# Where the rwkv operands are made beside gated linear attention: key norms, sigmoids, decays and the output gate moved

## The chip, the cores and the metric

The kernel runs on one core of a Trainium2 chip. The metric is the device time of one execution in microseconds (us). TensorE does the matrix products, VectorE (DVE) and ScalarE (ACT) the elementwise work, GpSimd (POOL) a few elementwise products, SyncE the loads of weights.

## The reference, cut to what matters

Two layers of attention and retention, a feed-forward block, a token mixer of four parts (pool, hgrn, rwkv, gla), and a second feed-forward block, over 512 tokens of 1024 features, all in float32. The change touches the token mixer, in the parts rwkv and gla:

```python
rr, rk, rv, xw, xa, xg = split(p_rw + (prev - p_rw) * rwkv_mu)
w_log = -softplus(-(rwkv_w0 + tanh(xw) @ rwkv_w2)) - 0.5
decay = exp(-exp(w_log))
a = sigmoid(rwkv_a0 + xa @ rwkv_a2)
g_r = sigmoid(xg) @ rwkv_g2
kk = split_heads(rk * rwkv_k_k)
kk = kk / maximum(sqrt(sum(kk * kk, -1)), 1e-12)
rk = rk * (1.0 + (a - 1.0) * rwkv_k_a)
# rwkv: S = S diag(decay) - (S kk)(kk * a)^T + v k^T, o = S r, token by token
# gla: o = chunked_gated_linear_attention(gq * scale, gk, gv, log_a), normed per head
y_gla = o_g * gla_norm * silu(gg)
```

The kernel computes the rwkv recurrence in chunks of 64 tokens, with the inverse of a triangular matrix per chunk and head. For it every key is scaled with the decays from the start of its chunk, which are exponentials of a running sum of `sigma`, the sigmoid of the low-rank product.

## The kernel before

Each engine has its own program; semaphores with names tie them. The order of the work is written out by hand. A weight arrives as a unit (512 or 384 KB) in one of 4 raw slots; ScalarE writes its high part (`w_high`, "weights high") and VectorE the rest (`w_low`, "weights split"), 3 slots each; `use()` keeps these splits 3 units ahead of the products. TensorE does three passes per product (L497 to L499).

The mixers' stage runs pool, hgrn and gla first. `linear_attention` (L840 on TensorE, L1591 on VectorE, L2267 on ScalarE) builds the scores of a chunked attention level by level, in `ORDER` = 32, 16, 8, 4, 2, 1, 64, 128, 256. For each level VectorE writes the logs of a factor (`logs`), ScalarE takes their exponential (`factor`), VectorE multiplies (`factors`), TensorE makes the scores (`scores`), and VectorE copies them with a mask (up to 64) or ScalarE copies them (`far`, levels 128 and 256). Between levels `fill(n)` does other work. Behind the last level come the mixed products, scores by values, whose results ScalarE lands in `y_gla`; then it presets X and XT, and the inverse begins.

In gla, `fill_gla` makes the eight rwkv projections between the first levels (0 to 5). VectorE lands each (`rwkv landed`) and mixes it with the token before (`rwkv mixed`), ScalarE keeps the own part (`rwkv own`). From the seventh fill on, `operand_steps` (L945, L1764, L2397) makes the rwkv operands: tanh, low-rank products, key squares and key norms; the four sigmoids; GpSimd's power -0.5 of the norms (L2657); the norms spread and turned; the scans of sigma (`cum`), the exclusive sum `cum - sigma`, three exponentials, and then `kkE`, `bI`, `kI` and `rE`. `bend_gate("gla")` (L2319) takes the silu of gla's output gate, between two exponentials.

`keep_busy(n)` makes n products that nobody reads. A PSUM bank is taken in turn out of 8; `take` waits until its user before is done.

Of the kernel before, what the change touches and what calls it, by code (L numbers as in the profile page):

```python
# [76 lines left out]
for _sem, _names in (  # L77
        ("rwkv operands by T", "sigma in,a gate in,gate out,key norm,key turned,bonus in,tokA turned,tokB turned"),
        ("rwkv operands by S", "rwkv tanh,rwkv sigmoid,sigma,a gate,g tok,key squares,key spread,rwkv exps,rwkv fades,bonus,tokA,tokB,"
                               "rwkv own,X preset,XT preset"),  # L80
        ("rwkv operands by V", "key floored,key scaled,sigma summed,sigma before,rE,rwkv landed,rwkv mixed"),
        ("inverse by T", "AT product,X product,A_ak product,Gv product,M_rk product,M_rb product,W1 product,"
                         "W2T product,X step,XT step,Pm product"),
        ("inverse by V", "X made,AT,X,XT made,A_ak,M_rk,M_rb,W2T"),
        ("inverse by S", "Pm,Gv,W1")):
    SHARED_BY.update((_name, _sem) for _name in _names.split(","))
# [103 lines left out]
class Memory:  # L190
# [80 lines left out]
    def mixers(self, region, rotary_at, xg_at, phase_at, end):  # L271
# [9 lines left out]
        m.y_tok = {name: r.room(f"y_{name}", TT, G) for name in ("hgrn", "rwkv", "gla")}  # L281
        first_at = r.at
# [167 lines left out]
def tensor_engine(e, s, mem, units):  # L450
# [371 lines left out]
    def mixers():  # L822
# [17 lines left out]
        def linear_attention(name, fill):  # L840
# [41 lines left out]
            for n in range(len(ORDER)):  # L882
                if n + 1 < len(ORDER):
                    fill(n + 1)
                if name == "gla" and n == len(ORDER) - 1:
                    keep_busy(3)
                scores(n)
# [57 lines left out]
        def operand_steps():  # L945
            yield
            for f in range(2):
                for what, r in (("sigma", slice(0, 64)), ("a gate", slice(64, 128))):
                    i = take((what, f), (what, f))
                    p.wait_ge(*of("rwkv tanh"))  # L950
                    group(banks[i][:, :], [(m.lora[r, 0, blk(f)], m.mixed[r, 6, :])], what + " in", f)
# [6 lines left out]
            yield  # L958
# [6 lines left out]
            for f in range(2):  # L965
                i = take(("key turned", f), ("key scaled", f))
                p.wait_ge(*of("key spread"))
                transposes(i, [flat(m.kI)[:, blk(2 * t + f)] for t in range(TT)], "key turned", f)
            yield
            yield  # L970
            yield

        projections, operand_prep = rwkv_steps(), operand_steps()

        def fill_gla(n):
            if n < 2:
                next(values_g)
                next(projections)
            elif n < 6:
                next(projections)  # L980
                if n in (2, 4):
                    next(projections)
                if n == 5:
                    p.mark("xg read", MIX_NORM)
            else:
                next(operand_prep)

        linear_attention("gla", fill_gla)
        for _ in operand_prep:
            pass  # L990
# [228 lines left out]
def vector_engine(e, s, mem, units):  # L1219
# [359 lines left out]
    def mixers():  # L1579
# [11 lines left out]
        def linear_attention(name, fill, mix):  # L1591
# [69 lines left out]
            def finish():  # L1661
                squares = groups_of(flat(k2 if name == "hgrn" else mem.square), G)
                v.wait_ge(*of("mixed landed", name, 1))
# [9 lines left out]
                v.wait_ge(*of("gate bent", name))  # L1673
                tt(y, y, v2[:, :, G:], ALU.mult, "y made", name)
# [68 lines left out]
        finish_hgrn = linear_attention("hgrn", fill_hgrn, lambda n: None)  # L1743
# [19 lines left out]

        def operand_steps():  # L1764
            yield
            norms = small[:, 176:192]
            v.wait_ge(*of("key norm"))
            ts(norms, bank("key norm")[:, 0:16], 1e-24, None, ALU.max, ALU.bypass, "key floored")
            yield
            v.wait_ge(*of("sigma", 1))  # L1770
            for f in range(2):
                scan(m.cum[:, f, :], m.sigma[:, f, :], "sigma summed", f)
            tt(m.tmp, m.cum, m.sigma, ALU.subtract, "sigma before")
# [4 lines left out]
            yield  # L1778
# [6 lines left out]
            yield  # L1785
# [6 lines left out]
            yield  # L1792
            tt(m.kI, rk, eI, ALU.mult, *STEP)
            v.wait_ge(*of("rwkv fades"))
            tt(m.rE, rr, m.eB, ALU.mult, "rE")
            yield

        projections, operand_prep = rwkv_steps(), operand_steps()

        def fill_gla(n):  # L1800
            if n < 6:
# [5 lines left out]
                if n in (2, 4):  # L1807
                    next(projections)
                    next(projections)
            else:  # L1810
                next(operand_prep)
# [5 lines left out]
        finish_gla = linear_attention("gla", fill_gla, mix_gla)  # L1817
        for _ in operand_prep:
            pass
# [3 lines left out]
    def inverse(m, finish_gla):  # L1823
# [37 lines left out]
        for size in (2, 4, 8, 16, 32):  # L1861
# [7 lines left out]
            for h in HEADS:  # L1869
# [4 lines left out]
                update("XT", m.XT[:, h, :], True, h)  # L1874
            next(side, None)
# [111 lines left out]
def scalar_engine(e, s, mem, units, t):  # L1987
# [273 lines left out]
    def mixers():  # L2261
# [5 lines left out]
        def linear_attention(name, fill):  # L2267
# [29 lines left out]
            for n in range(len(ORDER)):  # L2297
# [3 lines left out]
                elif name == "gla":  # L2301
                    fill(n + 1)
                scores(n)
            if name == "hgrn":
                fill(len(ORDER))
# [83 lines left out]
        def rwkv_steps():  # L2389
            for f in range(8):  # L2390
                use()
# [5 lines left out]
        def operand_steps():  # L2397
            a.wait_ge(*of("rwkv mixed", 7))
            act(m.mixed[0:64, 6, :], m.mixed[0:64, 6, :], "rwkv tanh", func=ACT.Tanh)
            a.wait_ge(*of("xg read", MIX_NORM))  # L2400
            for f in range(2):
                act(m.kI[:, f, :], m.mixed[:, 2 + f, :], "key squares", func=ACT.Square, scale=mem.col("rwkv_k_k", f))
            yield
            for f in range(2):
                for what, out, bias in (("sigma", m.sigma, "rwkv_w0"), ("a gate", m.a_gate, "rwkv_a0")):
# [3 lines left out]
            a.wait_ge(*of("key norm"))  # L2409
            a.wait_ge(*of("key inverse"))  # L2410
            act(heads(flat(m.kI)), small[:, 176:192].unsqueeze(2).to_broadcast([P, 16, 64]), "key spread")
            yield
# [4 lines left out]
            yield  # L2417
            a.wait_ge(*of("sigma before"))
            act(m.tmp, m.tmp, *STEP, func=ACT.Exp, scale=-HALF_E)
            act(m.rE, m.cum, "rwkv exps", func=ACT.Exp, scale=HALF_E)  # L2420
            act(m.eB, m.cum, "rwkv fades", func=ACT.Exp, scale=-HALF_E)
            yield
            yield

        projections, operand_prep = rwkv_steps(), operand_steps()

        def fill_gla(n):
# [5 lines left out]
            elif n < 6:  # L2433
                next(projections)
                if n in (2, 4):
                    next(projections)
            else:
                next(operand_prep)
            if n == 4:
                bend_gate("gla")  # L2440
# [8 lines left out]
        for _ in operand_prep:  # L2449
            pass  # L2450
# [5 lines left out]
    def inverse(m, finish_gla):  # L2456
# [21 lines left out]
        for size in (2, 4, 8, 16, 32):  # L2478
# [7 lines left out]
            for h in HEADS:  # L2486
                if h + 2 < 4:
                    product(h + 2)
                else:
                    next(side, None)  # L2490
            next(side, None)
# [85 lines left out]
def gpsimd_engine(e, s, mem, t):  # L2577
# [56 lines left out]
    def mixers():  # L2634
# [22 lines left out]
        tt(norms, norms, root, ALU.pow, "key inverse")  # L2657
        inverse(m)
# [208 lines left out]
```

## Time and profile before

| | us |
|---|---|
| median of 3 runs | 1688.22 |
| lowest and highest run | 1681.46, 1688.24 |
| profiled execution, its own time | 1687.16 |
| its span in the profile | 1685.2 |
| TensorE busy in the span | 1650.3 |
| VectorE busy | 861.3 |
| ScalarE busy | 669.0 |
| GpSimd busy | 124.7 |

The span runs from the first to the last instruction recorded; the time holds 1.96 us more. An engine is busy while it computes; what stands in square brackets at the end of a row is the time it stood idle just before, and who released it. Times within the trace count from the span's start. The stage of the change lies between 1090 and 1240 us.

### The profile page before, as it was taken

Reading aid. Unit: us, or ns where it says so; the run is one execution under the profiler, and the core shown is the slowest. Engines: PE = TensorE matmul, PEld = TensorE weight load, DVE = VectorE, ACT = ScalarE, POOL = GpSimd, SP = SyncE. Lnnn points to the kernel's source line nnn. Section 1 sums busy time; section 2 is a strip of 40 time slices with the busy share of each in tenths; the row PEclk is TensorE's granted clock in tenths of the full one; section 3 lists DMA queues with packets and bytes.
Section 4 is the critical chain, followed back from the end, with each engine's and each line's share of the span. In section 5 each row is a group of like instructions: output and inputs, shape, how many; then the busy total and the mean of one; then the engine's idle time right before and its main releaser. Section 6 shows DMA issues by size and latency. Waiting matters only on the chain.

```text
span 1685.2 us, 23809 instructions
## 1 busy us (share of the span) xinstructions
PE 1650.3 (98%) x9540; PEld 1338.2 (79%) x9540; DVE 861.3 (51%) x1170; ACT 669.0 (40%) x1017; POOL 124.7 (7%) x126
## 2 busy tenths in 40 slices
PE   9999999999999999999999999998999999999997
PEld 6877778877777888888888878887877888888886
DVE  6733445542444565444433478577556554444333
ACT  6145565314656433233222355346333433333221
POOL 0001001000100110000000310000410200000000
PEclk9999999999999999999999999997899999999999
DMA  5412212331221223332233422220002232232331
GB/s 180 154 63 76 88 51 88 113 125 63 75 77 53 98 85 103 100 101 90 88 103 94 141 76 63 63 66 18 3 23 86 88 101 92 96 97 85 103 98 56
DMA packets 40750, 144.14 MB, mean 86 GB/s; under 512 B 4816, under 2 KB 4832, under 8 KB 40256
## 3 DMA queue, kind: packets, MB, share of 16 engines
q1 hardware_dynamic: 37296, 131.61, 24.7%
q0 software_dynamic: 2192, 8.87, 1.6%
q10 hardware_dynamic: 1152, 2.14, 0.4%
q8 instruction: 76, 1.25, 0.3%
q14 instruction: 34, 0.28, 0.1%
HBM read 140.50 MB, written 2.10 MB: 85 GB/s over the span
## 4 chain that ended last, share of the span: by engine, by line
PE 85%; DVE 8%; ACT 5%; issue 1%; POOL 0%; DMA 0%; DVEq 0%; ACTq 0%; SPq 0%; POOLq 0%
PE bank L497 25%; PE bank L499 24%; PE bank L498 24%; PE bank L479 3%; PE bank L1017 2%; PE bank L485 1%; DVE sb_w_low L1230 1%; PE bank L664 1%; PE bank L728 1%; PE bank L707 1%; ACT sb_w_high L1999 1%; DVE sb_E L1230 1%; PE bank L862 1%; DVE sb_near L1644 1%; DMA sb_x<-xT 0%
## 5 line engine op out<-in xcount | busy, mean ns | idle before, releaser
L1230 DVE TENSOR_TENSOR sb_w_low<-sb_raw,sb_w_high 128x1024 fp32r<-128x1024 f32 (+1 forms) x253 | 310.9, 1229 | 368.0 <-ACT sb_w_high L1999 361.5
L497 PE MATMUL bank<-sb_xg_high,sb_w_high 128*128 128x512 f32 x1176 | 465.6, 396 | 2.0 <-DVE sb_w_low L1230 1.4
L499 PE MATMUL bank<-sb_xg_high,sb_w_low 128*128 128x512 f32 x1176 | 459.0, 390 | 0.0
L498 PE MATMUL bank<-sb_xg_low,sb_w_high 128*128 128x512 f32 x1176 | 458.5, 390 | 0.0
L1999 ACT ACTIVATE sb_w_high<-sb_raw 128x1024 fp32r<-128x1024 f32 (+1 forms) x253 | 263.3, 1041 | 349.1 <-PE bank L499 325.1
L497 PEld LDWEIGHTS bank<-sb_xg_high,sb_w_high 128*128 128x128 f32 x1176 | 221.1, 188 | 65.3 <-issue 15.8
L499 PEld LDWEIGHTS bank<-sb_xg_high,sb_w_low 128*128 128x128 f32 x1176 | 221.0, 188 | 47.1
L498 PEld LDWEIGHTS bank<-sb_xg_low,sb_w_high 128*128 128x128 f32 x1176 | 221.3, 188 | 44.3 <-issue 0.2
L499 PE MATMUL bank<-sb_h_high,sb_w_low 128*128 128x512 f32 x352 | 136.9, 389 | 0.0
L497 PE MATMUL bank<-sb_h_high,sb_w_high 128*128 128x512 f32 x352 | 136.9, 389 | 0.0
L498 PE MATMUL bank<-sb_h_low,sb_w_high 128*128 128x512 f32 x352 | 136.9, 389 | 0.0
L497 PE MATMUL bank<-sb_w_high,sb_xg_high 128*128 128x512 f32 x256 | 103.2, 403 | 0.0
L498 PE MATMUL bank<-sb_w_low,sb_xg_high 128*128 128x512 f32 x256 | 100.3, 392 | 0.0
L499 PE MATMUL bank<-sb_w_high,sb_xg_low 128*128 128x512 f32 x256 | 100.0, 391 | 0.0
L2586 POOL TENSOR_TENSOR sb_square_sum<-sb_square_sum,sb_square 128x512 f32<-128x512 f32 x20 | 26.1, 1307 | 748.4 <-ACT sb_square L1999 748.4
L499 PEld LDWEIGHTS bank<-sb_h_high,sb_w_low 128*128 128x128 f32 x352 | 66.1, 188 | 13.8
L498 PEld LDWEIGHTS bank<-sb_h_low,sb_w_high 128*128 128x128 f32 x352 | 66.1, 188 | 13.8
L497 PEld LDWEIGHTS bank<-sb_h_high,sb_w_high 128*128 128x128 f32 x352 | 66.1, 188 | 13.5
L1999 ACT ACTIVATE sb_h_high<-sb_up 128x512 fp32r<-128x512 f32 x44 | 27.8, 632 | 115.8 <-DVE sb_up L1230 115.8
L1230 DVE TENSOR_TENSOR sb_up<-bank,sb_inv_rms 128x512 f32<-128x512 f32 x44 | 30.4, 691 | 78.2 <-PE bank L499 77.4
L1999 ACT ACTIVATE sb_gate<-sb_gate 128x512 f32<-128x512 f32 x44 | 27.8, 632 | 92.3 <-DVE sb_gate L1230 92.3
L497 PEld LDWEIGHTS bank<-sb_w_high,sb_xg_high 128*128 128x128 f32 x256 | 48.3, 189 | 17.1 <-issue 7.1
(343 smaller groups left out, 1995.4 us busy)
## 6 DMA issues: line engine op xcount, KB each, us to landing
sb_raw<-w_ffn_in SPq DMA_DIRECT2D x88, 512.0 KB, 3.5
sb_raw<-w_ffn_out SPq DMA_DIRECT2D x32, 512.0 KB, 3.5
sb_raw<-w_tok SPq DMA_DIRECT2D x24, 512.0 KB, 3.5
sb_raw<-w_mix_f SPq DMA_DIRECT2D x18, 512.0 KB, 3.5
sb_raw<-w_rot SPq DMA_DIRECT2D x16, 512.0 KB, 3.6
sb_raw<-w_qk SPq DMA_DIRECT2D x16, 512.0 KB, 3.4
sb_raw<-w_out SPq DMA_DIRECT2D x16, 512.0 KB, 3.5
sb_raw<-w_ffn_out SPq DMA_DIRECT2D x16, 384.0 KB, 3.1
```

Of the source, the lines that this page charges most:

```text
L479: made = e.matmul(out, lhsT, rhs, start=n == 0, stop=n == len(pairs) - 1)
L485: made = e.transpose(banks[i][:, blk(n)], in_, mem.ident)
L497: e.matmul(out, w[0], v[0], start=first, stop=False)
L498: e.matmul(out, w[0], v[1], start=False, stop=False)
L499: return e.matmul(out, w[1], v[0], start=False, stop=last)
L664: made = e.matmul(out[k], m.feat["rk"][r, f, blk(j)], m.feat["rq"][r, f, j * P:], start=part == 0, stop=part == 1)
L707: e.matmul(out[k], m.qT[r, j, blk(q)], m.kT[r, j, 0:keys], start=True, stop=True).then_inc(*p.up("scores", n, 2 * j + k, q))
L728: made = e.matmul(out[64 * k:64 * k + 64, blk(q)], m.tok["av"][:, key, h * ATT_DIM:(h + 1) * ATT_DIM], m.probT[:, 2 * (q % 2) + k, blk(key ...
L1017: made = e.matmul(out(banks[i], t, c), left(t, c), right(t, c), start=True, stop=True)
L1230: e.tensor_tensor(out, a, b, op).then_inc(*v.up(*signal))
L1999: e.activation(out, in_, func, bias=bias, scale=scale, accum_out=accum).then_inc(*a.up(*signal))
L2586: e.tensor_tensor(out, a, b, op).then_inc(*g.up(*signal))
```

## The change

The operands are made at other places. Key squares, key norms and GpSimd's power move from the fills of levels 64 and 1 into the projections (fill 4), the spread to fill 5. They use the memory of `y_rwkv`. TensorE turns the keys just ahead of the scores of level 256, with two keep-busy products in place of three. All sigmoids, gla's output gate among them, stand in fill 6; its silu becomes a sigmoid on ScalarE and a product on GpSimd. The scans of sigma stand between the logs and the factors of level 128; the exclusive decay is the inclusive one of the token before, so that one subtraction and one exponential go and a small copy for the first token of each chunk comes. VectorE makes all the operands in fill 8. The products of rwkv's output gate go behind the scores of level 256. Two splits of weights move from projections 6 and 7 into the inverse, behind sizes 4 and 8 on VectorE, 2 and 4 on ScalarE.

```diff
@@ TensorE
-                if name == "gla" and n == len(ORDER) - 1:
-                    keep_busy(3)
+                if before_last and n == len(ORDER) - 1:
+                    before_last()
+                    keep_busy(2)
...
+        def key_norms():
             i = take(("key norm",), ("key floored",))
             p.wait_ge(*of("key squares"))
             for t in range(TT):
                 for f in range(2):
                     at = 4 * t + 2 * f
-                    group(banks[i][:, at:at + 2], [(m.kI[:, f, blk(t)], mem.table("same_head")[:, 0:P:64])], "key norm")
+                    group(banks[i][:, at:at + 2], [(m.key_sq[:, f, blk(t)], mem.table("same_head")[:, 0:P:64])], "key norm")
+
+        def turn_keys():
+            for f in range(2):
+                i = take(("key turned", f), ("key scaled", f))
+                p.wait_ge(*of("key spread"))
+                transposes(i, [flat(m.key_sq)[:, blk(2 * t + f)] for t in range(TT)], "key turned", f)
...
             elif n < 6:
                 next(projections)
+                if n == 4:
+                    key_norms()
                 if n in (2, 4):
                     next(projections)
...
+            elif n == 6:
+                low_rank_gates()
+            elif n == 9:
+                output_gate()
+
+        linear_attention("gla", fill_gla, turn_keys)
@@ VectorE
+                between(n)
                 if n + 1 < len(ORDER):
                     factors(n + 1)
                     fill(n + 1)
...
-                use()
+                if f < 6:
+                    use()
                 v.wait_ge(*of("rwkv", f))
...
+        def sum_sigmas(n):
+            if n == 6:
+                for f in range(2):
+                    v.wait_ge(*of("sigma", f))
+                    scan(m.cum[:, f, :], m.sigma[:, f, :], "sigma summed", f)
...
-            tt(m.tmp, m.cum, m.sigma, ALU.subtract, "sigma before")
...
+            v.wait_ge(*of("rwkv fades"))
+            tt(out[:, :, 1:], keys[:, :, 1:], fades[:, :, 0:CHUNK - 1], ALU.mult, *STEP)
+            ts(out[:, :, 0:1], keys[:, :, 0:1], 1.0, None, ALU.mult, ALU.bypass, *STEP)
             v.wait_ge(*of("a gate", 1))
             v.wait_ge(*of("rwkv exps"))
-            tt(m.kkE, kk, m.tmp, ALU.mult, *STEP)
...
+            elif n == 8:
+                operand_steps()
...
+            if size in (4, 8):
+                use()
@@ ScalarE
-            act(gate, gate, "gate bent", name, func=ACT.Sigmoid if name == "hgrn" else ACT.Silu)
+            if name == "hgrn":
+                act(gate, gate, "gate bent", name, func=ACT.Sigmoid)
+            else:
+                act(m.gate_sigmoid, gate, "gate sigmoid", func=ACT.Sigmoid)
...
+                if n == 5:
+                    low_rank_tanh()
+                    spread_norms()
                 next(projections)
+                if n == 3:
+                    square_keys()
...
+            elif n == 6:
+                sigmoids()
+            elif n == 7:
+                raise_decays()
+            elif n == 9:
+                land_gate()
...
+            if size in (2, 4):
+                use()
@@ GpSimd
         tt(norms, norms, root, ALU.pow, "key inverse")
+        gate = m.operands["gla"][3][:, :, G:]
+        g.wait_ge(*of("gate sigmoid"))
+        tt(gate, gate, m.gate_sigmoid, ALU.mult, "gate bent", "gla")
```

## Rows read from the trace of the kernel before

**Rows 1.** Span and busy totals of the page.

```profile
span 1685.2 us, 23809 instructions
...
PE 1650.3 (98%) x9540; PEld 1338.2 (79%) x9540; DVE 861.3 (51%) x1170; ACT 669.0 (40%) x1017; POOL 124.7 (7%) x126
```

**Rows 2.** Busy time per stretch: five engines, TensorE clock as share of 2.4 GHz, DMA.

```profile
1147.00:1149.00 2.00, 0.18 (x4) 0.04 (x2) 1.86 (x3) 0.92 (x2) 0.00 (x0) 0.86 0.08 29
...
1157.00:1165.00 8.00, 8.00 (x45) 7.04 (x45) 3.54 (x6) 6.17 (x8) 3.44 (x1) 0.50 0.01 2
...
1166.00:1171.00 5.00, 3.95 (x23) 2.03 (x22) 4.72 (x5) 2.78 (x6) 0.00 (x0) 1.00 0.01 2
...
1186.00:1189.00 3.00, 3.00 (x16) 3.00 (x16) 1.37 (x4) 2.43 (x6) 0.73 (x1) 0.50 0.00 0
...
1197.00:1203.00 6.00, 6.00 (x130) 6.00 (x132) 3.35 (x6) 1.14 (x3) 1.30 (x2) 0.50 0.01 3
```

**Rows 3.** TensorE in order of time, 1143 to 1175: start, duration, line, operation.

```profile
1143.39 3.79 PE L862 MATMUL bank<-sb_E 64*128 64x64 f32 x64
1150.21 3.78 PE L479 MATMUL bank<-sb_mixed,sb_lora 64*128 64x512 f32 x8 [3.03 <-ACT sb_mixed L1999]
1153.92 3.57 PE L479 MATMUL bank<-sb_mixer,sb_kI 128*128 128x2 f32 x16
...
1161.04 3.78 PE L479 MATMUL bank<-sb_lora,sb_mixed 128*128 128x256 f32 x8
...
1166.02 1.16 PE L873 MATMUL bank<-sb_E 64*128 64x128 f32 x16
1167.11 2.84 PE L813 MATMUL bank<-sb_inv_rms,sb_ones 128*128 128x512 f32 x6
1171.22 2.00 PE L876 MATMUL bank<-sb_E 64*128 64x256 f32 x16 [1.26 <-DVE sb_bI L1238]
```

**Rows 4.** Chain of work that ended last, 1157 to 1184: start, duration, what.

```profile
1157.88 3.45 POOL sb_small L2586
...
1174.27 8.89 PE bank L479 x80
```

**Rows 5.** TensorE in order of time, behind the mixed products.

```profile
1185.31 1.28 PE L479 MATMUL bank<-sb_mixer,sb_sigma 128*128 128x2 f32 x8
...
1192.01 0.38 PE L485 MATMUL bank<-sb_shared,sb_kkE 128*128 128x128 f32 x2
```

**Rows 6.** VectorE in order of time, 1134 to 1182.

```profile
1134.95 0.96 DVE L1230 TENSOR_TENSOR sb_w_low<-sb_raw,sb_w_high 128x768 fp32r<-128x768 f32 x1 [0.21 <-ACT sb_w_high L1999]
...
1142.29 1.53 DVE L1230 TENSOR_TENSOR sb_E<-sb_E,sb_kq_gla 128x1024 f32<-128x1024 f32 x1 [1.05 <-ACT sb_E L1999]
...
1144.99 0.69 DVE L1230 TENSOR_TENSOR sb_shifted<-bank,sb_inv_rms 128x512 f32<-128x512 f32 x1
...
1153.56 2.63 DVE L1644 COPY_PREDICATED sb_near<-sb_mixer,bank 128x512 f32<-128x512 int32 x2
...
1166.48 2.48 DVE L1250 TENSOR_TENSOR_SCAN sb_cum<-sb_mixer,sb_sigma 128x512 f32<-128x512 f32 x2
...
1170.32 1.60 DVE L1238 SCALAR_TENSOR_TENSOR sb_bI<-sb_mixed,sb_cols,bank 128x512 f32<-128x512 f32 x2
...
1181.66 1.23 DVE L1230 TENSOR_TENSOR sb_rE<-sb_mixed,sb_eB 128x1024 f32<-128x1024 f32 x1
```

**Rows 7.** ScalarE in order of time, around the output gate's silu.

```profile
1137.47 1.28 ACT L1999 ACT_TABLE_LOAD   x1
```

**Rows 8.** GpSimd in order of time, the inverse stage.

```profile
1225.85 2.35 POOL L2586 TENSOR_TENSOR sb_g_tok<-sb_g_tok,sb_rows 128x1024 f32<-128x1024 f32 x1
```

**Rows 9.** VectorE in order of time, while GpSimd builds pooling sums.

```profile
962.80 2.08 DVE L1230 TENSOR_TENSOR sb_w_low<-sb_raw,sb_w_high 128x1024 fp32r<-128x1024 f32 x1
...
967.55 1.23 DVE L1230 TENSOR_TENSOR sb_w_low<-sb_raw,sb_w_high 128x1024 fp32r<-128x1024 f32 x1 [1.87 <-ACT sb_w_high L1999]
```

**Rows 10.** GpSimd in order of time, the same stretch.

```profile
960.73 5.30 POOL L2586 TENSOR_TENSOR sb_s<-sb_s 128x1050 f32<-128x1050 f32 x3
```

More of the change, by code:

```diff
@@ L80 @@
                                "rwkv own,X preset,XT preset"),
-        ("rwkv operands by V", "key floored,key scaled,sigma summed,sigma before,rE,rwkv landed,rwkv mixed"),
+        ("rwkv operands by V", "key floored,key scaled,sigma summed,rE,rwkv landed,rwkv mixed"),
         ("inverse by T", "AT product,X product,A_ak product,Gv product,M_rk product,M_rb product,W1 product,"
@@ L281, in mixers @@
         m.y_tok = {name: r.room(f"y_{name}", TT, G) for name in ("hgrn", "rwkv", "gla")}
+        m.key_sq = flat(m.y_tok["rwkv"]).rearrange("p (f n) -> p f n", f=2)
+        m.gate_sigmoid = self.square.rearrange("p f (a b) -> p (f a) b", b=G)
         first_at = r.at
@@ L943, in rwkv_steps @@
                 yield
[L945 to L951, printed above, removed]
+        def key_norms():
             i = take(("key norm",), ("key floored",))
@@ L956, in operand_steps, with low_rank_gates, output_gate @@
                     at = 4 * t + 2 * f
-                    group(banks[i][:, at:at + 2], [(m.kI[:, f, blk(t)], mem.table("same_head")[:, 0:P:64])], "key norm")
-            yield
+                    group(banks[i][:, at:at + 2], [(m.key_sq[:, f, blk(t)], mem.table("same_head")[:, 0:P:64])], "key norm")
[4 more added lines that the diff above has]
+                transposes(i, [flat(m.key_sq)[:, blk(2 * t + f)] for t in range(TT)], "key turned", f)
+        def low_rank_gates():
+            for what, r in (("sigma", slice(0, 64)), ("a gate", slice(64, 128))):
+                for f in range(2):
+                    i = take((what, f), (what, f))
+                    p.wait_ge(*of("rwkv tanh"))
+                    group(banks[i][:, :], [(m.lora[r, 0, blk(f)], m.mixed[r, 6, :])], what + " in", f)
+        def output_gate():
             for half in range(2):
@@ L964, in operand_steps @@
                           "gate out", half)
[L965 to L973, printed above, removed]
+        projections = rwkv_steps()
         def fill_gla(n):
@@ L984, in fill_gla @@
                     p.mark("xg read", MIX_NORM)
[L985 to L990, printed above, removed]
+            elif n == 6:
[3 more added lines that the diff above has]
+        linear_attention("gla", fill_gla, turn_keys)
         p.mark("TensorE at", "inverse")
@@ L1589, in mixers, with linear_attention @@
             tt(m.p_in[:, f, m.pad:], bank("pool in", f)[:, :], mem.inv_rms, ALU.mult, "pool in landed", f)
-        def linear_attention(name, fill, mix):
+        def linear_attention(name, fill, mix, between):
             q2, k2, c2, v2 = m.operands[name]
@@ L1662, in finish @@
                 squares = groups_of(flat(k2 if name == "hgrn" else mem.square), G)
+                v.wait_ge(*of("gate bent", name))
                 v.wait_ge(*of("mixed landed", name, 1))
@@ L1672, in finish @@
                 tt(split(y), split(y), ms.unsqueeze(2).to_broadcast([P, n_norms, width]), ALU.mult, *STEP)
-                v.wait_ge(*of("gate bent", name))
                 tt(y, y, v2[:, :, G:], ALU.mult, "y made", name)
@@ L1762, in mixers, with floor_norms @@
         rr, rk, kk, eI = m.mixed[:, 0:2, :], m.mixed[:, 2:4, :], m.bI, m.rE
-        def operand_steps():
[L1765 to L1772, printed above, removed]
-            tt(m.tmp, m.cum, m.sigma, ALU.subtract, "sigma before")
+        def floor_norms():
+            v.wait_ge(*of("key norm"))
+            ts(small[:, 176:192], bank("key norm")[:, 0:16], 1e-24, None, ALU.max, ALU.bypass, "key floored")
+        def sum_sigmas(n):
+            if n == 6:
+                for f in range(2):
+                    v.wait_ge(*of("sigma", f))
+                    scan(m.cum[:, f, :], m.sigma[:, f, :], "sigma summed", f)
+        def operand_steps():
             for f in range(2):
@@ L1791, in operand_steps @@
                 stt(m.sigma[:, f, :], rr[:, f, :], mem.col("rwkv_r_k", f), rk[:, f, :], ALU.mult, ALU.mult, *STEP)
-            yield
             tt(m.kI, rk, eI, ALU.mult, *STEP)
-            v.wait_ge(*of("rwkv fades"))
             tt(m.rE, rr, m.eB, ALU.mult, "rE")
-            yield
-        projections, operand_prep = rwkv_steps(), operand_steps()
+        projections = rwkv_steps()
         def fill_gla(n):
@@ L1808, in fill_gla @@
                     next(projections)
+                    if n == 4:
+                        floor_norms()
                     next(projections)
-            else:
-                next(operand_prep)
+            elif n == 8:
+                operand_steps()
         def mix_gla(n):
@@ L1815, in mix_gla @@
                 next(projections)
-        finish_gla = linear_attention("gla", fill_gla, mix_gla)
-        for _ in operand_prep:
-            pass
+        finish_gla = linear_attention("gla", fill_gla, mix_gla, sum_sigmas)
         inverse(m, finish_gla)
@@ L2300, in linear_attention @@
                     fill(n + 1)
-                elif name == "gla":
-                    fill(n + 1)
                 scores(n)
-            if name == "hgrn":
-                fill(len(ORDER))
+            fill(len(ORDER))
             for half in range(2):
@@ L2390, in rwkv_steps @@
             for f in range(8):
-                use()
+                if f < 6:
+                    use()
                 a.wait_ge(*of("rwkv landed", f))
@@ L2395, in rwkv_steps, with square_keys, low_rank_tanh, spread_norms @@
                 yield
-        def operand_steps():
+        def square_keys():
+            a.wait_ge(*of("rwkv mixed", 3))
+            for f in range(2):
+                act(m.key_sq[:, f, :], m.mixed[:, 2 + f, :], "key squares", func=ACT.Square, scale=mem.col("rwkv_k_k", f))
+        def low_rank_tanh():
+            a.wait_ge(*of("rwkv mixed", 6))
+            act(m.mixed[0:64, 6, :], m.mixed[0:64, 6, :], "rwkv tanh", func=ACT.Tanh)
+        def spread_norms():
+            a.wait_ge(*of("key norm"))
+            a.wait_ge(*of("key inverse"))
+            act(heads(flat(m.key_sq)), small[:, 176:192].unsqueeze(2).to_broadcast([P, 16, 64]), "key spread")
+        def sigmoids():
             a.wait_ge(*of("rwkv mixed", 7))
-            act(m.mixed[0:64, 6, :], m.mixed[0:64, 6, :], "rwkv tanh", func=ACT.Tanh)
             a.wait_ge(*of("xg read", MIX_NORM))
[L2401 to L2405, printed above, removed]
+            for what, out, bias in (("sigma", m.sigma, "rwkv_w0"), ("a gate", m.a_gate, "rwkv_a0")):
+                for f in range(2):
                     a.wait_ge(*of(what + " in", f))
@@ L2408, in operand_steps, with raise_decays, land_gate @@
             act(m.mixed[:, 7, :], m.mixed[:, 7, :], "rwkv sigmoid", func=ACT.Sigmoid)
[L2409 to L2412, printed above, removed]
+            bend_gate("gla")
+        def raise_decays():
+            a.wait_ge(*of("sigma summed", 1))
+            act(m.eB, m.cum, "rwkv fades", func=ACT.Exp, scale=-HALF_E)
+            act(m.rE, m.cum, "rwkv exps", func=ACT.Exp, scale=HALF_E)
+        def land_gate():
             for half in range(2):
@@ L2416, in operand_steps @@
                     "g tok", half)
[L2417 to L2425, printed above, removed]
+        projections = rwkv_steps()
         def fill_gla(n):
@@ L2433, in fill_gla @@
             elif n < 6:
+                if n == 5:
+                    low_rank_tanh()
+                    spread_norms()
                 next(projections)
+                if n == 3:
+                    square_keys()
                 if n in (2, 4):
                     next(projections)
[L2437 to L2440, printed above, removed]
+            elif n == 6:
[4 more added lines that the diff above has]
+                land_gate()
         def preset(name, out, behind):
@@ L2448, in mixers @@
         finish_gla = linear_attention("gla", fill_gla)
-        for _ in operand_prep:
-            pass
         preset("X", m.X, "factors read")
@@ L2490, in inverse @@
                     next(side, None)
+            if size in (2, 4):
+                use()
             next(side, None)
```

8 lines of the change are left out of this document (4 added, 4 removed).

## The prediction

> **What bounds the kernel.** I read the page first. TensorE is busy 98% of a span of 1685.2 us [rows 1], so a stretch can give time only where TensorE waits, or where its clock is low. Second the table of stretches: behind the last rwkv projection the busy share drops and the granted clock falls to half, 1.2 GHz, and is back at 2.4 GHz from 1166 on [rows 2]. Two later stretches, at 1186 and at 1197, are at half as well. Third TensorE in order of time [rows 3]: the last projection ends at 1143.4, the scores of levels 2 and 1 end at 1147.2, and then TensorE stands 3.03 us for ScalarE's tanh; everything up to 1165 runs at half rate. The scores of level 256, which every mixed product needs, start at 1171.22. Fourth the chain of waits [rows 4]: it doesn't run through those matrix products. It goes through VectorE's logs, copies and factors, through GpSimd's power of the key norms (3.45 us), ScalarE's spread of them, VectorE's scans and key scaling, and from 1171 on through TensorE: the mixed products take 8.89 us from 1174.27 to 1183.2. So the measure of this change is when the mixed products start. What follows them (two landings, the presets of X and XT, the masks, the inverse) hangs on their end, before and after.
>
> **The dense stretch.** Sixteen key-norm products now stand between rwkv projections 5 and 6. They took 3.57 us at half clock [rows 3]; eight of the same shape take 1.28 us partly at full clock [rows 5], so I count 16 x 0.145 = 2.3 us. Nothing hides them, as TensorE has no gap there: the last projection ends at 1143.4 + 2.3 = 1145.7. The inputs are in time (projection 3 is mixed two levels before, ScalarE's two squares take a gap before the next exponential), and GpSimd's 3.45 us now lie under projections 6 and 7. VectorE comes to the landing of projection 7 at 1144.99 [rows 6]. Two splits of 0.96 us go, and the wait of 1.05 us for ScalarE at 1142.29 goes too: it was the output gate's silu between two table loads of 1.28 us [rows 7], of which one pair is saved. VectorE is then ready sooner, and the landing is at 1145.75, set by TensorE. This first part costs 0.76 us on VectorE's line.
>
> **VectorE up to the last levels.** From there VectorE does what it did before, so the copies of level 1, which began at 1153.56 and took 2.63 [rows 6], end at 1156.2 + 0.76 = 1157.0. Now the scans of sigma stand next: 2.48 us [rows 6], which before lay behind the factors of level 256. ScalarE has both sigmas by 1153, because the four sigmoids come right behind the exponential of level 64 and one table load. The factors of level 128 end at 1157.5 + 0.76 + 2.5 = 1160.8 without any contention. ScalarE's two decay exponentials (1.06 each) lie under VectorE's next log and copies, one exponential and the subtraction that made the exclusive sum (1.22) are gone, and the factors of level 256 end at 1165.2, where they ended at 1166.4.
>
> **GpSimd's new product.** The gate times its sigmoid has the size of the 2.35 us product in the inverse [rows 8]. It starts when ScalarE's sigmoids end, near 1156.4, and runs over the start of the scans, which read two tiles in SBUF. What does that cost? A split of VectorE over GpSimd's sums took 2.08 us instead of 1.23, and another, 5 us later, under other GpSimd products, took its 1.23 [rows 9, 10]. So the bounds are nothing and the rest of the product, 1156.4 + 2.35 - 1157.0 = 1.75 us. I take 1.7, since the scan would find the product already running, as the slow split did, and keep both ends. The factors of level 128 then end at 1162.5. The Trainium skill, SBUF - State Buffer, section Who interferes with whom, states that a VectorE instruction with two SBUF inputs contends with a GpSimd instruction that reads SBUF, and that the second to issue blocks entirely. By that the scan loses the full 1.75 us; the slow split agrees, the fast one doesn't show it. No term hangs on this sentence.
>
> **TensorE's tail.** Before the scores of level 128 it has now nothing to do for some 6 us (level 64's scores end near 1155), since the gate products went behind level 256. Behind the 3.03 us wait of before the clock was at half [rows 2, 3], so the tail restarts at 1.2 GHz. Its work from the factors of level 128 to the mixed products, at 2.4 GHz: scores 1.16 and 2.00, three keep-busy products at 2.84 / 3 = 0.95 [rows 3], eight transposes at 0.11 (they start 0.22 us apart in pairs at full clock; the row's 0.38 holds overlap) [rows 5], and the output gate, 3.78 at half, 1.9 at full [rows 3]. That is 1.16 + 2.00 + 2.85 + 0.9 + 1.9 = 8.8 us. From 1162.5 it is done at 1171.3 if the clock were full throughout. While it is at half, half of the time is lost. Before, the clock came back some 15 us after the restart at 1150.2, but behind 3.6 us of key norms with two columns each; now the transposes and keep-busy products follow at once. I take 5 us at half, so 2.5 lost: the mixed products start at 1173.8 against 1174.27, a gain of 0.5. The bounds are no loss, and half the 8.8 us done twice over, +8.8.
>
> No semaphore takes more: the key scaling no longer frees a bank that level 256 waits for (it did, to 1171.1 [rows 3, 6]), the transposes stand just before it and take banks of level 1, emptied by 1157. VectorE's operand work, 12.57 us from 1170.32 to 1182.9 [rows 6], starts at 1167 and loses 0.5 of waiting; the product for the first token of each chunk adds 0.2. It ends near 1179.5, before the mixed products do, so it stays hidden. If that cover were gone, each us would count.
>
> **The inverse.** Two splits of 0.96 us come behind sizes 4 and 8, and two of ScalarE's behind 2 and 4. ScalarE waits a us or more in these places. VectorE's first one comes before two masks and a step; TensorE has side products there. I count 0.3, between 0 and 1.9. The loads for the unit ring start 70 us later, and their first reader is behind 1250; in between the queue has nothing else. Free.
>
> **Sum.** -0.5 + 0.3, rounded to nothing: the time of the profiled execution was 1687.16, 1.96 above its span; I predict 1687.2. That is 1.0 under the median of the three runs, 1688.22, whose lowest is 1681.46: executions of one kernel differ by more than this change. Half a per cent, 8.4 us, is about what a measurement of this kernel can tell from no change.
>
> **Rivals.**
> Early clock: no contention and the clock back within a us of the restart. The mixed products start at 1160.8 + 8.8 + 0.5 = 1170.1, -4.2: 1683.3. For it: the fast split. Against it: the clock needed the whole of 1150 to 1165. Chance 0.2.
> Clock lost in the dense stretch: the key norms feed two columns per product, like the bonus sums at 1184 to 1186, behind which the clock was at half with TensorE busy [rows 2, 5]. A few us of projections at half cost 1.7, and with 3 us more of low tail, 1.5: 1690.5. Against it: scores of 2 us between projections never lowered the clock. Chance 0.17.
> Later stretches healed: the 3.4 us around 1186 and the 6.8 around 1197 to 1203 at half [rows 2] depend on where a change of level falls. If shifting the stage heals both, 5 us, and early clock comes with it, 1678.5. Nothing in the profile speaks for both at once. Chance 0.1.
> Slower: the clock stays at half from the restart through the mixed products. The tail then takes 8.8 more, and 8.89 of mixed products up to twice as long, together up to 17: 1696 to 1704. It decides from the point where the whole tail and nothing of the mixed products runs at half. For it: before, 15 us passed at half. Against it: the keep-busy products are dense. Chance 0.08.
> The forecast, between 1685 and 1689.5: chance 0.45.
>
> **Numbers.** The likeliest gives 1687.2. The range reaches from the middle between the early clock and healed stretches, 1680, to 1692.5, just beyond the lost clock; outside lie the slow case and most of the healed one. Faster by over 0.5% is the healed case and a little of the early one, 0.12; slower the slow case, 0.08; the same 0.80.
>
> **What would show it.** Key norms in a dense stretch at 2.3 us; one pair of table loads fewer; no wait for GpSimd's power; a first scan longer than 1.24 us beside a GpSimd product; TensorE idle 5 us or more before level 128; half clock behind it; mixed products starting between 1172 and 1175. The prediction is wrong if VectorE's operands end behind the mixed products, if a bank wait stands before level 256, or if the clock stays high over the gap.

## The result, and the profile after

| | us | ratio to before |
|---|---|---|
| before, median of 4 runs | 1688.23 | 1 |
| after, median of 4 runs | 1702.98 (1700.45 to 1703.59) | 1.0094 [1.0082, 1.0107] |
| predicted | 1687.2 (1680.0 to 1692.5) | |

The change makes the kernel slower by 0.9%. The page of the changed kernel: the span grew by 13.4 us, TensorE's busy time by 1.1 [rows 1].

```profile
span 1698.6 us, 23804 instructions
...
PE 1651.4 (97%) x9538; PEld 1342.3 (79%) x9538; DVE 862.0 (51%) x1170; ACT 665.4 (39%) x1014; POOL 127.3 (7%) x127
```

The chain of waits (start, duration, what) says where it went.

```profile
1154.37 2.72 DVE sb_cum L1256
...
1157.18 1.24 DVE sb_cum L1256
...
1176.61 17.33 PE bank L481 x80
1193.94 1.06 PE bank L1014 x32
```

It goes through the two scans of sigma and the rest of VectorE's operands into the mixed products, x80. They start at 1176.61, 2.3 later than before, and take 17.33 instead of 8.89 [rows 4]. So they end 10.8 later, and the small products behind them, at half clock too, bring the first landing of the inverse to 1210.15 instead of 1196.52, 13.6 later. Behind it nothing changed: from there to the end of the span it is 488.4 us, 488.7 before.

The stage itself lost more than these differences say. This execution of the changed kernel came to gla's first products 2.3 us sooner than that of the kernel before, ahead of the first block that was moved (from 900 to 1088 us the mean granted clock was 1.00, before 0.98). Of each pair, the first row is of the kernel before:

```profile
1088.71 2.37 PE L849 MATMUL bank<-sb_kq_gla 64*128 64x128 f32 x32
1086.45 2.33 PE L851 MATMUL bank<-sb_kq_gla 64*128 64x128 f32 x32
...
1196.52 0.86 ACT L1999 ACTIVATE sb_Pm<-bank 128x256 f32<-128x256 f32 x2
1210.15 0.86 ACT L2008 ACTIVATE sb_Pm<-bank 128x256 f32<-128x256 f32 x2
```

Counted from these first products, the mixed products start 4.8 us later (90.2 instead of 85.4) and the inverse's first landing comes 15.9 later (123.7 instead of 107.8).

TensorE in order of time: start, duration, line (two to six higher than before), and in brackets the idle time and who ended it.

```profile
1127.96 1.84 PE L481 MATMUL bank<-sb_mixer,sb_y_rwkv 128*128 128x2 f32 x16
...
1159.79 2.08 PE L875 MATMUL bank<-sb_E 64*128 64x128 f32 x16 [7.65 <-DVE sb_E L1236]
...
1165.19 2.00 PE L878 MATMUL bank<-sb_E 64*128 64x256 f32 x16
...
1168.08 1.89 PE L481 MATMUL bank<-sb_lora,sb_mixed 128*128 128x256 f32 x8
1176.61 2.40 PE L481 MATMUL bank<-sb_v_gla,sb_near 128*128 128x64 f32 x10 [6.64 <-DVE sb_rE L1236]
```

The last row is the one to read. TensorE has finished the output gate's products at 1170.0 and stands for 6.64 us, released by VectorE's `rE`, the last of the rwkv operands. The mixed products read none of them. The table of stretches (busy time of TensorE, its weight loads, VectorE, ScalarE, GpSimd, then the granted clock) shows the price that follows: in this second wait the clock falls to 1.2 GHz, and it is still at that level from 1190 to 1195.

```profile
1155.00:1160.00 5.00, 0.21 (x2) 0.22 (x4) 4.76 (x4) 2.73 (x4) 0.99 (x1) 0.50 0.00 0
1160.00:1165.00 5.00, 5.00 (x28) 3.73 (x28) 4.62 (x6) 3.38 (x7) 0.00 (x0) 0.68 0.00 0
...
1170.00:1175.00 5.00, 0.00 (x0) 0.00 (x0) 4.79 (x7) 0.60 (x1) 0.00 (x0) 0.84 0.00 2
1175.00:1180.00 5.00, 3.39 (x16) 3.39 (x17) 1.52 (x2) 0.00 (x0) 0.00 (x0) 0.50 0.00 0
...
1190.00:1195.00 5.00, 5.00 (x52) 4.76 (x51) 0.00 (x0) 0.99 (x2) 0.00 (x0) 0.50 0.00 0
```

The first wait, 7.65 us ahead of level 128, put the clock at half as well, but it was back before 1165, as the second row shows. VectorE and GpSimd:

```profile
1135.44 0.69 DVE L1236 TENSOR_TENSOR sb_shifted<-bank,sb_inv_rms 128x512 f32<-128x512 f32 x1 [2.39 <-PE bank L501]
...
1143.05 0.69 DVE L1236 TENSOR_TENSOR sb_shifted<-bank,sb_inv_rms 128x512 f32<-128x512 f32 x1 [0.70 <-PE bank L501]
...
1154.37 4.03 DVE L1256 TENSOR_TENSOR_SCAN sb_cum<-sb_mixer,sb_sigma 128x512 f32<-128x512 f32 x2
1158.51 1.22 DVE L1236 TENSOR_TENSOR sb_E<-sb_E,sb_kq_gla 128x1024 f32<-128x1024 f32 x1
...
1162.92 1.23 DVE L1236 TENSOR_TENSOR sb_E<-sb_E,sb_kq_gla 128x1024 f32<-128x1024 f32 x1
...
1175.33 1.22 DVE L1236 TENSOR_TENSOR sb_rE<-sb_mixed,sb_eB 128x1024 f32<-128x1024 f32 x1
```

```profile
1133.14 2.93 POOL L2610 TENSOR_TENSOR sb_small<-sb_small 128x16 f32<-128x16 f32 x1 [157.18 <-DVE sb_small L1240]
1153.64 2.35 POOL L2610 TENSOR_TENSOR sb_v_gla<-sb_v_gla,sb_square 128x1024 f32<-128x1024 f32 x1 [17.57 <-ACT sb_square L2008]
```

The scans take 4.03 instead of 2.48 [rows 6], beside a GpSimd product from 1153.64 to 1155.99, the gate's. VectorE's operands end at 1176.55.

What makes TensorE wait is a name in the unchanged part of VectorE's `linear_attention`:

```python
            for n in range(len(ORDER)):
                ...
                if n + 1 < len(ORDER):
                    factors(n + 1)
                    fill(n + 1)
            v.mark("near done", name)
```

`mark` gives a name to whatever VectorE signalled last. Before, that was the step of the operands that stood in fill 8: the two scans, the subtraction and the key scaling. After, fill 8 holds all of them, so "near done", for which the mixed products wait, means `rE` done. The diff doesn't touch the line.

### The profile page after: what moved, and what is told of

Its sections match the earlier page's. It is cut to its first block, busy times and chain, and to the rows that moved or that the text cites. A ratio compares the mean times of both kernels' runs of the same rounds, so it can differ in the third digit from the quotient of the medians.

```text
span 1698.6 us, 23804 instructions
## 1 busy us (share of the span) xinstructions
PE 1651.4 (97%) x9538; PEld 1342.3 (79%) x9538; DVE 862.0 (51%) x1170; ACT 665.4 (39%) x1014; POOL 127.3 (7%) x127
## 4 chain that ended last, share of the span: by engine, by line
PE 88%; DVE 7%; ACT 3%; issue 1%; DMA 0%; DVEq 0%; SPq 0%; ACTq 0%
PE bank L499 25%; PE bank L501 25%; PE bank L500 25%; PE bank L481 4%; PE bank L1023 2%; PE bank L487 2%; PE bank L666 1%; PE bank L730 1%; PE bank L709 1%; PE bank L864 1%; ACT sb_w_high L2008 1%; DVE sb_w_low L1236 1%; DVE sb_E L1236 1%; DMA sb_x<-xT 0%; PE bank L588 0%
```

## The experiments

Each ratio is to the kernel before, run on the same chip (median 1685.68 for the first four, 1684.89 for the others); the changed kernel's own 1.0094 is from the first measurement, with four runs of each kernel.

| kernel | median us | ratio [95%] |
|---|---|---|
| e1_mark_at_copies | 1684.40 | 0.9989 [0.9979, 0.9999] |
| e2_busy_wait | 1691.48 | 1.0034 [1.0022, 1.0047] |
| e3_before_late_mark | 1706.17 | 1.0119 [1.0102, 1.0136] |
| e4_mark_silu | 1682.47 | 0.9980 [0.9969, 0.9991] |
| e5_gate_early | 1682.11 | 0.9982 [0.9973, 0.9991] |
| e6_gap_busy | 1680.18 | 0.9971 [0.9960, 0.9983] |
| e7_inverse_busy | 1679.03 | 0.9968 [0.9955, 0.9980] |
| e8_splits_back | 1682.93 | 0.9989 [0.9980, 0.9998] |

The last four were measured on another chip than the first four, so ratios are compared across them, not medians. The profiled executions come to gla at different times, from 1085.9 to 1089.5. So their traces are compared by times counted from gla's first products: to the start of the mixed products, and to the first landing of the inverse (`sb_Pm`). The last columns are the time from that landing to the end of the span, and the mean granted clock in the 60 us behind it. Times are in us, and each row is one execution.

| kernel | mixed products | first landing | from there on | clock |
|---|---|---|---|---|
| before | 85.4 | 107.8 | 488.7 | 0.94 |
| after | 90.2 | 123.7 | 488.4 | 0.94 |
| e1_mark_at_copies | 84.7 | 107.1 | 488.5 | 0.94 |
| e2_busy_wait | 90.2 | 112.7 | 487.6 | 0.97 |
| e3_before_late_mark | 94.3 | 127.3 | 487.6 | 0.94 |
| e4_mark_silu | 82.6 | 105.0 | 487.6 | 0.97 |
| e5_gate_early | 80.7 | 103.1 | 491.1 | 0.89 |
| e6_gap_busy | 81.1 | 104.7 | 485.7 | 1.00 |
| e7_inverse_busy | 81.1 | 103.6 | 485.7 | 1.00 |
| e8_splits_back | 83.5 | 106.0 | 487.0 | 0.97 |

**The signal alone, on the changed kernel.**

```diff
                 if n:
                     scores(n - 1)
+                    if ORDER[n - 1] == 64:
+                        v.mark("near done", name)
                 between(n)
...
-            v.mark("near done", name)
```

> The changed kernel, but VectorE's signal 'near done' is tied to the last masked copy (level 64) and no longer to whatever VectorE did last before the end of the loop, so that the mixed products of gla don't wait for the rwkv operands. Theory (the wait for the operands, then the clock it lets fall): the mixed products start right behind the output gate's products, at about 1170.0 instead of 1176.6, take 8.9 us instead of 17.3, and the time is about 1684 (1681 to 1687), ratio to before 0.995 to 0.999. Rival (the clock falls anyway, because of the 7.65 us gap before level 128): start at 1170, but 12 to 17 us long, 1690 to 1695, ratio 1.002 to 1.005.

TensorE of this kernel:

```profile
1160.92 2.08 PE L875 MATMUL bank<-sb_E 64*128 64x128 f32 x16 [7.65 <-DVE sb_E L1236]
...
1170.56 1.89 PE L481 MATMUL bank<-sb_lora,sb_mixed 128*128 128x256 f32 x8
1172.28 1.22 PE L481 MATMUL bank<-sb_v_gla,sb_near 128*128 128x64 f32 x10
...
1181.25 0.69 PE L1014 MATMUL bank<-sb_kkE,sb_bI 64*64 64x64 f32 x32
```

No wait stands before the mixed products; they run from 1172.28 to 1181.2, 9.0 long. The median is 1684.40 and the ratio 0.9989, as the theory said: 1.05% under the changed kernel, some 17.7 us, by moving one name (16.6 by the first landing in the traces). The start is later than I wrote because this execution runs 1.1 later as a whole and the clock came back later in the tail, in the keep-busy products. That is the tail's half clock which the prediction had priced; it costs about a us, not the loss.

**The wait without the clock.** Seven keep-busy products fill it; it is not taken away.

```diff
             fill(len(ORDER))
+            if name == "gla":
+                keep_busy(7)
             last = len(ORDER) - 1
```

> The changed kernel with seven keep-busy products, 0.95 us each, put into TensorE's wait before the mixed products; the wait itself stays. It tells the wait's own price from that of the clock. Theory: mixed products still start at 1176.6 to 1177, now at 2.4 GHz and 8.9 us long, so they end near 1185.6, 2.4 behind before; 1689 to 1692, ratio 1.000 to 1.003, that is 8 to 13 below the changed kernel. Rival (the clock was lost for another reason, the wait's filling doesn't matter): 1700 to 1703, ratio 1.008 to 1.010.

```profile
1171.07 6.17 PE L815 MATMUL bank<-sb_inv_rms,sb_ones 128*128 128x512 f32 x14
1177.76 1.30 PE L481 MATMUL bank<-sb_v_gla,sb_near 128*128 128x64 f32 x10 [0.51 <-DVE sb_rE L1238]
...
1186.80 0.69 PE L1016 MATMUL bank<-sb_kkE,sb_bI 64*64 64x64 f32 x32
```

The mixed products start as late as in the changed kernel (0.51 us of waiting is left, for `rE`), but they take 9.0 us. Ratio 1.0034, just above the expected range. Between this and the changed kernel lies 0.60%, 10 us: the clock. Between this and e1_mark_at_copies lies 0.45%, 7.6 us: the wait. The traces, by the first landing, give 11.0 and 5.6. Both say that more than half of the loss is the clock that the wait let fall; the intervals of the ratios alone don't settle which part is larger, but each part is clear of them.

**The signal alone, on the kernel before.**

```diff
-            v.mark("near done", name)
+            if name == "hgrn":
+                v.mark("near done", name)
             fill(len(ORDER))
...
         for _ in operand_prep:
             pass
+        v.mark("near done", "gla")
         inverse(m, finish_gla)
```

> The kernel before, with nothing of the change but gla's 'near done' moved behind the last rwkv operand, as the change did without saying so. Theory: mixed products wait for rE, to 1182.9 instead of 1174.3 (8.6 us), and restart at half clock: 8.6 for the wait, up to 8.4 for the products and 3 behind them, 1700 to 1709, ratio 1.008 to 1.013. Rival (something else of the change makes it slow): 1686 to 1690, ratio 0.999 to 1.001.

```profile
1183.43 2.37 PE L479 MATMUL bank<-sb_v_gla,sb_near 128*128 128x64 f32 x10 [7.08 <-issue]
...
1200.66 1.13 PE L1008 MATMUL bank<-sb_kkE,sb_bI 64*64 64x64 f32 x32
```

With nothing of the change but the late signal, the kernel before waits 7.1 us, makes its mixed products from 1183.4 to 1200.7 at half clock, and is 1.2% slower. That is more than with the whole change, though the two intervals overlap a little (1.0102 to 1.0107). The traces say what the rest of the change gives back: with it the operands are ready sooner, and the mixed products start 90.2 us behind gla's first products instead of 94.3.

**GpSimd's product beside the scan.** e1_mark_at_copies with the gate's silu on ScalarE again, now behind the sigmoids.

```diff
-            if name == "hgrn":
-                act(gate, gate, "gate bent", name, func=ACT.Sigmoid)
-            else:
-                act(m.gate_sigmoid, gate, "gate sigmoid", func=ACT.Sigmoid)
+            act(gate, gate, "gate bent", name, func=ACT.Sigmoid if name == "hgrn" else ACT.Silu)
...
-        g.wait_ge(*of("gate sigmoid"))
-        tt(gate, gate, m.gate_sigmoid, ALU.mult, "gate bent", "gla")
```

> As e1_mark_at_copies, and gla's output gate is a silu on ScalarE again, behind the sigmoids, with its table load, and without the product on GpSimd. Theory of contention: the first scan of sigma takes 1.24 us again instead of 2.8, ScalarE's exponential of level 128 comes 1.28 later and then sets the factors, at 1158.9 instead of 1159.7: 0.5 to 1 us less than e1_mark_at_copies. Rival (the long scan has another cause): it stays at 2.8 and the time is 0 to 1.3 above e1_mark_at_copies.

VectorE of this kernel:

```profile
1156.26 2.55 DVE L1256 TENSOR_TENSOR_SCAN sb_cum<-sb_mixer,sb_sigma 128x512 f32<-128x512 f32 x2
1159.45 1.23 DVE L1236 TENSOR_TENSOR sb_E<-sb_E,sb_kq_gla 128x1024 f32<-128x1024 f32 x1 [0.64 <-ACT sb_E L2009]
```

The two scans are back at 2.55 us, 1.5 less, and VectorE now waits 0.64 us for ScalarE's exponential behind the further table load. The theory's durations hold. The time is 0.09% lower than e1_mark_at_copies, 1.5 us, but the two intervals overlap, so for the time this is no more than likely. The mixed products start 2.1 us sooner, of which 1.1 is not VectorE's: TensorE's four keep-busy matmuls ran at full clock here (1.92) and not in e1_mark_at_copies (3.04).

**The output gate in the gap.** e4_mark_silu, its products ahead of level 128.

```diff
-            elif n == 9:
+            elif n == 8:
                 output_gate()
...
             elif n == 7:
                 raise_decays()
-            elif n == 9:
                 land_gate()
```

> As e4_mark_silu, and the output gate's eight products stand ahead of the scores of level 128, in TensorE's gap of 6.7 us, with their landing behind ScalarE's decay exponentials. Theory (what is left of the wait is TensorE's tail of products before the mixed ones, so each product out of it counts): the mixed products start 1.7 us sooner than in e4_mark_silu, at 1169.2, and the time falls by 1 to 2.5, to 1680 to 1681.5. Rival (VectorE's factors or ScalarE's far copies bound the tail now): the start moves by less than 0.5 and the time by nothing.

First TensorE of e4_mark_silu, then of this kernel:

```profile
1144.84 2.00 PE L864 MATMUL bank<-sb_E 64*128 64x64 f32 x32
...
1152.04 2.00 PE L864 MATMUL bank<-sb_E 64*128 64x64 f32 x32 [1.64 <-DVE sb_E L1236]
1160.73 2.08 PE L875 MATMUL bank<-sb_E 64*128 64x128 f32 x16 [6.69 <-DVE sb_E L1236]
...
1170.96 1.22 PE L481 MATMUL bank<-sb_v_gla,sb_near 128*128 128x64 f32 x10
```

```profile
1153.40 3.34 PE L481 MATMUL bank<-sb_lora,sb_mixed 128*128 128x256 f32 x8
1158.48 1.16 PE L875 MATMUL bank<-sb_E 64*128 64x128 f32 x16 [1.74 <-DVE sb_E L1236]
1160.76 1.44 PE L487 MATMUL bank<-sb_shared,sb_y_rwkv 128*128 128x128 f32 x8 [1.12 <-DVE sb_near L1650]
...
1166.73 1.22 PE L481 MATMUL bank<-sb_v_gla,sb_near 128*128 128x64 f32 x10
```

From the start of level 128's scores to the mixed products it is 8.25 us instead of 10.23, as the theory said, although a new wait of 1.12 us for a bank (level 64's copies) takes some back. The gain reaches the inverse: its first landing comes 1.9 us sooner behind gla's first products. The masks make the transposes and the second group of products wait 0.5 and 0.8 us, but they did so in e4_mark_silu too (0.7 and 0.8). The time didn't follow: 0.9982 against 0.9980. What took the gain back lies behind the landing, 491.1 us instead of 487.6, with a lower clock, 0.89 instead of 0.97. First e4_mark_silu, then this kernel:

```profile
1193.00:1253.00 60.00, 55.69 (x1385) 50.07 (x1385) 34.32 (x81) 21.17 (x46) 22.07 (x24) 0.97 0.10 29
1189.00:1249.00 60.00, 56.55 (x1367) 51.98 (x1368) 32.05 (x74) 21.00 (x46) 21.91 (x24) 0.89 0.08 23
```

So the theory's mechanism is seen and its time is a miss. Whether the edit lowers the clock there, or only this execution had it lower, no run shows.

**The gap kept busy.** e5_gate_early with `keep_busy(4)` behind the output gate's products.

> As e5_gate_early, with four keep-busy products behind the output gate's in the same gap. Theory (the gap still drops the clock, and the first products behind it run at 1.2 GHz): scores of level 128, transposes and keep-busy at full rate, the tail shorter by 0.5 to 1.5, bounded by VectorE's factors of level 256 at 1165; time 0 to 1.5 below e5_gate_early. Rival (they make the scores of level 128 late): 0 to 1 above.

```profile
1156.40 3.60 PE L815 MATMUL bank<-sb_inv_rms,sb_ones 128*128 128x512 f32 x8
1159.93 1.44 PE L875 MATMUL bank<-sb_E 64*128 64x128 f32 x16
...
1166.96 1.22 PE L481 MATMUL bank<-sb_v_gla,sb_near 128*128 128x64 f32 x10
```

The scores of level 128 start at 1159.93 and the mixed products 7.03 later. But the four products make those scores late, as the rival said: the mixed products start 0.4 us later behind gla's first products than in e5_gate_early, not sooner. Ratio 0.9971 against 0.9982, some 1.9 us, but the intervals overlap from 0.9973 to 0.9983: not settled. In the trace nothing of it comes from the tail: the first landing is 1.5 us later, and what follows it is 5.4 us shorter, at a clock of 1.00 instead of 0.89.

**The inverse's wait kept busy.** e6_gap_busy, and two keep-busy products before the first updates.

```diff
             product(0)
             product(1)
+            if size == 2:
+                keep_busy(2)
             for h in HEADS:
```

> As e6_gap_busy, with two keep-busy products in the wait of 2.6 us before the first updates of the inverse. Theory (this wait is what puts the first 3 to 7 us of the inverse at half clock, in the kernel before too): the clock stays at 2.4 GHz there, 1.5 to 3 us less than e6_gap_busy, 1677 to 1680. Rival (the keep-busy products come late themselves, or the low level comes from the small products): no difference, or 0.5 to 1 more.

```profile
1190.75 1.98 PE L815 MATMUL bank<-sb_inv_rms,sb_ones 128*128 128x512 f32 x4
1193.46 0.66 PE L1024 MATMUL bank<-sb_Pm,sb_XT 64*64 64x32 f32 x16 [0.73 <-ACT sb_Pm L2012]
```

The wait is 0.73 instead of 2.27 in e6_gap_busy, and the clock stays up behind it. But the expected 1.5 to 3 us are not there: 0.9968 against 0.9971. In e6_gap_busy's own profile the clock had stayed up behind this wait too, having fallen a few us earlier, among the transposes. The table has both at 1.00 and 485.7 us from the first landing on. Where the clock falls moves, so a fixed price for this wait was wrong. It has the lowest median of the study, 0.3% under before, though it is not separable from the one without the two products.

**The splits back.** e4_mark_silu with the two splits behind projections 6 and 7.

> As e4_mark_silu, with the two splits of weights back behind projections 6 and 7, where the kernel before had them. Theory (they were free in the inverse and cost VectorE 0.96 each in the projections, of which the gaps before the landings of projections 6 and 7, 2.4 and 0.7 us, hide the first and most of the second): 0 to 1 us above e4_mark_silu. Rival (in the inverse they delay the masks): 0 to 1 us below it.

```profile
1144.78 2.00 PE L864 MATMUL bank<-sb_E 64*128 64x64 f32 x32
...
1153.16 2.20 PE L864 MATMUL bank<-sb_E 64*128 64x64 f32 x32 [2.83 <-DVE sb_E L1236]
1161.87 2.08 PE L875 MATMUL bank<-sb_E 64*128 64x128 f32 x16 [6.50 <-DVE sb_E L1236]
```

From level 2's scores to level 128's it is 17.09 us, against 15.89 in e4_mark_silu; the wait before level 64 is 2.83 instead of 1.64. So the splits cost VectorE's line 1.2 us there. Of these 0.9 are left at the first landing, and from there on this execution is 0.6 us shorter, so the traces don't show that moving them paid. In time it is 0.9989 against 0.9980, again with intervals that overlap.

## Why the prediction was wrong, point by point

**The step that failed.** "No semaphore takes more": I looked for waits in banks and in the key scaling, and left out the wait for "near done". I even reckoned that the operands end near 1179.5, "before the mixed products do, so it stays hidden", when the mixed products can't begin before them. By my own numbers they would have started at 1179.5, 5 us later than before, behind a wait of 5.7 us, where 3.03 us of waiting had already been followed by half clock [rows 2, 3]. Measured: operands ready at 1176.55, a wait of 6.64 us, and the products 17.33 us long. My sign for this, operands that end behind the mixed products, couldn't appear, because the products wait for them. Shown by e1_mark_at_copies (taking the signal back removes the loss) and by e3_before_late_mark (adding it alone makes the loss).

**The slow rival.** Its time, 1696 to 1704, held by luck; its mechanism did not. It had the clock low from the restart at level 128. That low level ended by itself, in the changed kernel before 1165; the mixed products ran at half because of a second wait that I hadn't foreseen.

**The dense stretch.** Key norms at full clock: 1.84 us, I had 2.3. VectorE landed projection 7 at 1143.05, set by TensorE as forecast, and not at 1145.75; 2.3 of the difference is this execution's earlier arrival. Counted from gla's first products the landing comes 0.3 us later than before, where I had 0.76. The clock didn't fall in the dense stretch, so that rival is out for these executions. GpSimd's power (2.93) and the gate's sigmoid on ScalarE are off the chain, as forecast.

**VectorE's line.** From the landing of projection 7 to the end of level 1's copies it is 11.2 us before and after. The scans lost 1.55 us to GpSimd's product, I had 1.7. The Trainium skill, SBUF - State Buffer, section Who interferes with whom, has the second of two such instructions wait for the first; the trace agrees: 1153.64 + 2.35 is 1155.99, and the first scan, due at 1154.37, ends 1.10 behind that, against some 1.2 for its own work. Why the split at 967.55 took its usual 1.23 us beside GpSimd's work [rows 9] stays open.

**The tail.** From level 128's scores to the end of the gate's products: 10.2 us; I had 8.8 and 2.5 for the clock. In order of size right. Where the mixed products don't wait, in e1_mark_at_copies, they start 0.7 us sooner than before behind gla's first products; I had 0.5. The operand work took 12.3, as I had.

**The inverse.** The cost of two splits in it, which I put at 0.3, was not measured by itself. Leaving them in the projections costs 1.2 us on VectorE's line, and e8_splits_back leaves open which place is better for the time.

With the signal put right the change gives 0.1% (0.9989), with the silu back on ScalarE 0.2%: nearly the "nothing" of the forecast. The parts that I had sized were off by a us or so each, partly against each other.

## What to carry to other kernels

When work is moved in front of a point at which an engine's last instruction is given a name, everybody who waits for that name waits for the moved work too: list for each moved block which later names resolve to it, not only which banks and tiles it touches. Tie such a signal to the instruction that makes the data. And price a new wait of TensorE with what it does to the clock of the products behind it: here a wait of 6.64 us cost 5.6 to 7.6 us by itself and 10 to 11 more through the clock, and filling it with unread products alone gave those back. An edit of a us or two in such a stage can vanish in what the clock does behind it, so look at the granted clock of the following stretch before calling it useless.

## What the runs showed of the hardware that was not expected

A busy TensorE stayed at half clock. In the changed kernel the clock fell to 1.2 GHz in the wait of 6.64 us and stayed there through 17.33 us of 64-column products with TensorE hardly idle between them, and on to about 1204. Behind the wait of 7.65 us it was back at 2.4 GHz some 3.3 us after the restart at 1159.79 (in e1_mark_at_copies some 6 after 1160.92); what ran there were level 128's scores, transposes and the keep-busy products. A scan with two inputs in SBUF stood still for a GpSimd product: 4.03 us for the pair instead of 2.55. And the clock behind the stage differed between kernels that run nearly the same work there: 0.89 to 1.00 over 60 us, with 491.1 to 485.7 us from the inverse's first landing to the end of the span.
